# Experts of a routed mixture by items of 64 slots: one item at a time, with rows gathered and scattered per item by GpSimd, in place of rounds of two items side by side

## The chip, the cores and the metric

One core of a Trainium2 chip runs the whole program in one launch. The metric is the device time of that launch in microseconds (us), as the median over repeated runs. All arithmetic is in float32.

## The reference, cut to what matters

The program is four layers: two of one block (three attention and scan branches), then two of a second block, each of which ends in a hierarchical mixture of experts (MoE). The change lies in the two MoE stages, except for one piece of preparation in an attention stage of the first block.

```python
def hier_moe(h, wr_g, br_g, wr_e, br_e, w_gate, w_up, w_down):      # 512 tokens of 1024
    p_group = softmax(xf @ wr_g + br_g);  g_sel = top_k(p_group, 1)        # 4 groups
    fine = (xf @ wr_e + br_e)[chosen group]                                # 8 experts a group
    e_val, e_sel = top_k(fine, 2);  gate = p_top * softmax(e_val)
    ...
    y = (silu(x_rows @ w_gate[e]) * (x_rows @ w_up[e])) @ w_down[e]        # 1024->512, 512->1024
    out[token] += y * gate                                                 # 2 experts a token
x = x + g2 * hier_moe(h, ...)
```

There are 32 experts in a layer, each with three weight matrices of 2 MiB: 96 matrices, 201.3 MB, for each of the two MoE layers. A layer has 512 x 2 = 1024 pairs of token and expert. The reference's own inputs decide how they fall: in the first MoE layer expert 26 gets 69 pairs, expert 29 gets 135 and no other more than 64; in the second only expert 13 has more than 64 (67). In pieces of 64 ("items"), with at least one for each expert, that is 35 items in the first layer (two for expert 26, three for 29) and 33 in the second (two for expert 13).

## The kernel before, in words

A stage of the program is a block in which each of the five engines (TensorE, VectorE, ScalarE, GpSimd, and SyncE, which only issues DMA) runs its own instruction list; a barrier ends it. The MoE of a layer is two stages, `experts` and `moe_residual` (function `experts`).

In `experts`, SyncE first issues six 2 MiB loads (L2898: gate, up and down weights of experts 0 and 1). Meanwhile `route` (VectorE, with two ScalarE exponentials) turns the router's logits into choices, and `plan` ranks the pairs within each expert with TensorE and VectorE and writes a small table `counts` into SBUF, from which each engine later reads loop bounds and expert numbers into registers (`value_load`). The first rows are gathered on TensorE by a product with a one-hot matrix (L427, `pick`). At L2908 GpSimd scatters all token rows, eight indirect DMAs of 128 rows of 4 KB, into the tensor `expert_rows` in device memory, at the seat of each pair.

Then `item_experts` works in rounds. A round has two seats of 64 slots: even experts take seat 0, odd experts seat 1, one after the other, and an expert with more than 64 pairs keeps its seat for further rounds. The number of rounds is the longer of the two seats: 18 in the first MoE layer and 17 in the second. Each seat has its own buffer for gate, up and down weights. A round on TensorE is: gate product of both seats side by side in the two halves of bank 0 (`side_by_side`, L2796), up product into bank 1, transposes of the next round's rows (L2788), transposes of the hidden rows (L2811), down product into banks 4 and 5 (L2796, `experts_wd`). ScalarE does silu (L2840) and moves transposed rows (L2836, L2845), VectorE multiplies (L2861) and scales the result (L2868). SyncE issues the next round's gate loads when the gate product is done, and so on for up and down (L2744), and loads the 128 rows of the next round but one (L2736). GpSimd stores the 128 result rows of 4 KB (L2771) and waits for them to land.

In `moe_residual` GpSimd fetches the results back in token order with eight indirect DMAs of 128 rows (L2927), and VectorE adds them to `x`, weighted (L2952), and makes the next norm (L548, L549, and L2968 in the last layer, which needs the gain `g` loaded at L2939).

Since seats may be partly empty, `expert_rows` is filled with zeros once, by 32 DMAs of 512 KB that GpSimd issues in the first layer's fox attention (L694). In that stage TensorE also computes side products (L726) from weights `side_w` that SyncE loads (L708) into two buffers.

## Time and profile before

| | us |
|---|---|
| median of 3 runs (range) | 4008.1 (4007.0 to 4009.63) |
| the profiled execution's span, first to last instruction | 4008.1 |
| first MoE layer, both stages, about | 2309 to 2909 |
| second MoE layer, both stages, about | 3432 to 4008 |
| TensorE busy over the span | 3480.4 (87%) |

The profiled execution's span is the same as the median, so no time lies around the span that the sum would have to add. A busy share is an average over stages with different limits. The DMA line of the page (mean busy share of the 16 DMA engines, in 40 slices of 100.2 us) shows where transfers are the limit; the MoE stages are the slices 24 to 28 and 35 to 40.

### The profile page before, as it was taken

The page shows a single profiled execution, that of the slowest core. Times are in us where ns is not written, and L with a number is a line of the kernel's source. Part 1 is how long each engine was busy: PE and PEld are TensorE (multiplying, and loading weights), DVE is VectorE, ACT ScalarE, POOL GpSimd, SP SyncE. Part 2 cuts the span into 40 slices and gives each one's busy share as a digit, 9 for nine tenths or more (in the row PEclk, how much of TensorE's full clock was granted, in tenths as well). Part 3 has the DMA queues.
Part 4 walks back from the last instruction along what each step waited for, and adds up shares of the span by engine and source line. Part 5 has one row for each costly group of instructions (what it writes and reads, how often), then busy time and mean ns, then how long its engine had stood idle before and what let it go on. Part 6 is the DMA issues. An engine that isn't in the chain of part 4 may idle for free. (4 is left out here: it accounts for less than half of the span.)

```text
span 4008.1 us, 38008 instructions
## 1 busy us (share of the span) xinstructions
PE 3480.4 (87%) x13936; PEld 1752.2 (44%) x13937; DVE 1688.1 (42%) x3091; ACT 701.3 (17%) x1412; POOL 196.3 (5%) x263
## 2 busy tenths in 40 slices
PE   8998999888899999889889977778699978788775
PEld 4454434885444444378634432223243344422222
DVE  3235556775232555567548420000238766200002
ACT  1132204000112330310010100000122243100001
POOL 0001010001000001000000000000100130000000
PEclk9999999999999999899889989999889989799998
DMA  3115452004121226200143099999533421799996
GB/s 105 68 48 209 143 169 60 1 1 144 47 89 32 68 83 208 55 11 1 59 175 122 0 396 429 428 428 399 202 105 121 110 73 62 310 429 419 429 428 283
DMA packets 208086, 696.40 MB, mean 174 GB/s; under 512 B 22248, under 2 KB 105704, under 8 KB 182608
## 3 DMA queue, kind: packets, MB, share of 16 engines
q1 hardware_dynamic: 178576, 589.56, 38.4%
q0 software_dynamic: 29376, 105.05, 7.2%
q8 instruction: 85, 1.39, 0.2%
q14 instruction: 49, 0.40, 0.0%
HBM read 636.28 MB, written 58.28 MB: 173 GB/s over the span
## 5 line engine op out<-in xcount | busy, mean ns | idle before, releaser
L345 PE MATMUL bank<-fm,w 128*128 128x512 f32 (+1 forms) x912 | 397.3, 596 | 11.4 <-DMA w<-in_ab_w_in 6.3
L2796 PE MATMUL bank<-experts_wu,experts_hs 128*64 128x512 f32 x1120 | 275.8, 650 | 75.0 <-DMA experts_wu<-in_moe_w_up 75.0
L2796 PE MATMUL bank<-experts_wg,experts_hs 128*64 128x512 f32 x1120 | 272.2, 642 | 60.1 <-DMA experts_wg<-in_moe_w_gate 45.6
L345 PE MATMUL bank<-w,fm 128*128 128x512 f32 (+2 forms) x768 | 315.5, 567 | 6.5 <-DMA w<-in_w_in 6.5
L2861 DVE TENSOR_TENSOR fm<-bank,fm 128x512 f32<-128x512 f32 x35 | 37.0, 1056 | 638.9 <-PE bank L2796 638.9
L2796 PE MATMUL bank<-experts_wd,fm 128*64 128x512 f32 x1120 | 256.4, 611 | 45.4 <-issue 24.0
L345 PEld LDWEIGHTS bank<-fm,w 128*128 128x128 f32 (+1 forms) x912 | 172.4, 190 | 234.1 <-issue 221.0
L726 PE MATMUL bank<-fm,side_w 128*128 128x512 f32 x512 | 252.4, 619 | 6.9 <-DMA side_w<-in_w_in 5.4
L345 PEld LDWEIGHTS bank<-w,fm 128*128 128x128 f32 x768 | 142.2, 195 | 179.2 <-issue 153.8
L2796 PEld LDWEIGHTS bank<-experts_wu,experts_hs 128*64 128x64 f32 x1120 | 85.9, 148 | 263.2 <-issue 166.1
L2796 PEld LDWEIGHTS bank<-experts_wg,experts_hs 128*64 128x64 f32 x1120 | 94.6, 147 | 233.6 <-issue 230.5
L2868 DVE TENSOR_TENSOR fm<-bank,mod 128x512 f32<-128x512 f32 x70 | 45.1, 686 | 328.3 <-PE bank L2796 328.3
L427 PE MATMUL bank<-fm,w 128*128 128x512 f32 x384 | 170.3, 599 | 1.6 <-ACT rwkv_a L1362 1.6
L2796 PEld LDWEIGHTS bank<-experts_wd,fm 128*64 128x64 f32 x1120 | 83.7, 140 | 195.7 <-issue 168.3
L843 ACT ACTIVATE prob<-bank,nmax 128x128 f32<-128x128 f32 (+2 forms) x192 | 111.4, 580 | 219.6 <-DVE nmax L891 146.9
L726 PEld LDWEIGHTS bank<-fm,side_w 128*128 128x128 f32 x512 | 91.5, 197 | 91.3 <-issue 83.9
L1944 DVE SCALAR_TENSOR_TENSOR ada_sums<-ada_w,cond,ada_sums 128x1024 f32<-128x1024 f32 x84 | 105.8, 1282 | 37.1 <-DMA ada_w<-in_ada_w 35.9
L2840 ACT ACTIVATE fm<-bank 128x512 f32<-128x512 f32 x35 | 20.9, 597 | 560.2 <-PE bank L2796 560.2
L345 PE MATMUL bank<-w,merged 128*128 128x512 f32 x256 | 113.2, 600 | 3.1 <-DVE merged L1443 3.1
L427 PEld LDWEIGHTS bank<-fm,w 128*128 128x128 f32 x384 | 73.7, 193 | 96.3 <-issue 93.8
L345 PE MATMUL bank<-o_fm,w 128*128 128x512 f32 x240 | 105.8, 600 | 6.3 <-DMA w<-in_w_pc 6.3
L761 PE MATMUL bank<-consts,prob 128*128 128x128 f32 x512 | 78.7, 282 | 30.0 <-ACT pT L826 15.9
(484 smaller groups left out, 4875.5 us busy)
## 6 DMA issues: line engine op xcount, KB each, us to landing
experts_wg<-in_moe_w_gate SPq DMA_DIRECT2D x64, 2048.0 KB, 19.5
experts_wu<-in_moe_w_up SPq DMA_DIRECT2D x64, 2048.0 KB
experts_wd<-in_moe_w_down SPq DMA_DIRECT2D x64, 2048.0 KB
ada_w<-in_ada_w POOLq DMA_DIRECT2D x96, 512.0 KB, 4.9
w<-in_w_in SPq DMA_DIRECT2D x40, 512.0 KB, 3.9
expert_rows<-fm POOLq DMA_DIRECT2D x35, 512.0 KB, 10.3
fm<-expert_rows SPq DMA_DIRECT2D x33, 512.0 KB, 21.6
w<-in_w_in SPq DMA_DIRECT2D x16, 1024.0 KB, 7.2
```

Of the source, the lines that this page charges most:

```text
L345: ins = pe.matmul(bank, lhsT, rhs, start=(n == 0), stop=(n == len(todo) - 1))
L427: last = pe.matmul(out, lhsT, rhs, start=(n == 0), stop=(n == len(pairs) - 1))
L726: last = pe.matmul(SIDE[:, :], side_w[n % 2][:, k_, :], side_h[:, k_, :], start=(k_ == 0), stop=(k_ == DC - 1))
L761: last = pe.transpose(T[n % 2][:, j * P:(j + 1) * P], prob[s % 4][:, j * P:(j + 1) * P], chip.ident)
L843: act.activation(prob[s % 4][:, 0:n], S[s % n_scores][:, 0:n], ACT.Exp, bias=nmax[:, s:s + 1], scale=1.0 if bias is None else -1.0, accum_ ...
L1944: ins = dve.scalar_tensor_tensor(sums, self.slot[n % self.slots][:, :], by, sums, ALU.mult, ALU.add)
L2796: ins = pe.matmul(bank[rows, :], lhs[:, k, rows], weights[:, s, k, cols], start=(k == 0), stop=(k == chunks - 1))
L2840: act.activation(act_out[:, :], B[0][:, :], ACT.Silu).then_inc(*silued.inc())
L2861: dve.tensor_tensor(dealt(hid[:, :], FC), B[1][:, :].rearrange("p (q k) -> p q k", k=FC), act_out[:, :].rearrange("p (q k) -> p q k", k=FC ...
L2868: ins = dve.tensor_tensor(y[:, cols], B[4 + d][:, :], gate_row[:, cols], ALU.mult)
```

## The change

The two seats are given up. Work goes item by item, in the order of the experts, and an item's gate and up products run side by side in the two halves of bank 0, with the same rows as the stationary operand. Its down product comes one item late: in iteration `p` TensorE turns the hidden rows of item `p - 1`, makes gate and up of item `p`, turns the rows of item `p + 1`, and makes the down product of item `p - 1`, whose two column halves lie side by side in bank 4. Gate and up weights have two buffers each, down weights one. SyncE's list is written out for all 32 experts.

GpSimd gathers each item's rows from `token_rows` (the normed tokens, stored there by SyncE in the stage ahead, `keep`) with an indirect DMA of half rows (2 KB), and scatters the results as half rows straight to `made_rows`, in the order of the pairs. Slots without a pair are sent out of bounds (one slot of each half stays), so nothing is moved for them. GpSimd waits for no landing in its loop; VectorE does, before it overwrites `y`. `plan` makes the two index tables `at_from` and `at_to` in place of the scatter positions; the one-hot gather and the zero fill are gone. `moe_residual` reads `made_rows` with eight plain DMAs on SyncE, ahead of the clearing of semaphores and the load of `g`.

```diff
@@ attention (fox attention, first layer)
-                for n in range(cleared_rows.shape[0] // P):
-                    pool.dma_start(cleared_rows[n * P:(n + 1) * P, :], zero[:, :]).then_inc(*wiped.inc(16))
-                pool.wait_ge(*wiped.at(wiped.total))
@@ the stage ahead of experts
+    def keep(self, sp, h):
+        for t in range(TILES):
+            sp.wait_ge(*self.norm.normed.at(t + 1))
+            sp.dma_start(self.chip.token_rows[t * P:(t + 1) * P, :], h[:, t, :]).then_inc(*self.chip.tokens_kept.inc(16))
@@ plan
+            dve.tensor_tensor(at_slot[:, :, half * SLOTS:(half + 1) * SLOTS], over(chip.number, [P, 2 * TILES, SLOTS], 1),
+                              over(own_rank, [P, 2 * TILES, SLOTS], 2), ALU.is_equal)
+        link(dve.tensor_tensor(at_item[:, :, :], over(chip.number[:, 0:ITEMS], [P, 2 * TILES, ITEMS], 1),
+                               over(own_first, [P, 2 * TILES, ITEMS], 2), ALU.is_equal))
+        link(dve.tensor_tensor(at_item[:, :, :], at_item[:, :, :], over(chip.pair_number, [P, 2 * TILES, ITEMS], 2), ALU.mult))
...
+        product(pe, B[3][:, 0:ITEMS], [(at_slot[:, a, :], at_item[:, a, :]) for a in range(2 * TILES)]).then_inc(*tabled.inc())
@@ item_experts, SyncE
+        for e in range(EXPERTS):
+            if e == 2:
+                sp.wait_ge(*counted.at(1))
+            if e >= 2:
+                sp.wait_ge(*first_done.at(at(e - 2, END_AT, 1)))
+            load("moe_w_gate", e, wg[:, e % 2], gate_loaded[e % 2])
+            load("moe_w_up", e, wu[:, e % 2], up_loaded[e % 2])
+            if e == 0:
+                load_down(0)
+            if e >= 2:
+                sp.wait_ge(*down_done.at(at(e - 1, FIRST_AT, 1) + 1))
+                load_down(e - 1)
+        sp.wait_ge(*down_done.at(at(EXPERTS - 1, FIRST_AT, 1) + 1))
+        load_down(EXPERTS - 1)
@@ item_experts, GpSimd
-            pool.wait_ge(*yready.at(p + 1))
-            pool.dma_start(rows[bass.ds(p * P, P), :], y[:, :]).then_inc(*ystored.inc(16))
-            pool.wait_ge(*ystored.at(16 * p + 16))
-            pool.sem_inc(yfree.sem, 1)
+        with pool.Fori(2, n + 2) as q:
+            pool.wait_ge(*rows_turned.at(q - 1))
+            fetch(q - 1, picked_from, q)
+            pool.wait_ge(*y_ready.at(q))
+            pick_to(q - 2)
+            spread(q)
@@ item_experts, TensorE
+        def gate_and_up(p, s):
+            pe.wait_ge(*filled.at(p + 1))
+            for k in range(DC):
+                rows = hs[:, k % 4, k // 4, :]
+                for half, w in ((slice(0, SLOTS), wg), (upper, wu)):
+                    ins = pe.matmul(B[0][half, :], rows, w[:, s, k, :], start=(k == 0), stop=(k == DC - 1))
+            ins.then_inc(*first_done.inc())
...
+                with pe.Fori(first, end) as p:
+                    landed = pe.value_load(counts[0:1, bass.ds(p + DOWN_AT, 1)], min_val=16, max_val=16 * EXPERTS)
+                    turn_hidden(p)
+                    pe.wait_ge(*gate_loaded[s].at(16 * j + 16))
+                    pe.wait_ge(*up_loaded[s].at(16 * j + 16))
+                    gate_and_up(p, s)
+                    turn(p + 1)
+                    pe.wait_ge(*down_loaded.at(landed))
+                    down(p)
@@ item_experts, VectorE
+            dve.wait_ge(*down_done.at(p + 1))
+            dve.wait_ge(*y_stored.at(16 * p + 16))
+            dve.tensor_tensor(y[:, :], B[4][:, :], gate_half[:, :], ALU.mult).then_inc(*y_ready.inc())
@@ experts
+                @st.block.scalar
+                def _(act):
+                    for half in range(2):
+                        rows = slice(half * SLOTS, (half + 1) * SLOTS)
+                        act.activation(gate_half[rows, :], mod[rows, 5, half * BANK:(half + 1) * BANK], ACT.Copy).then_inc(*gated.inc())
                 route(chip, st, lg, choice, weight, routed, routed_ready)
@@ moe_residual
-                    pool.indirect_dma_start(out=rows[:, at, :], out_offset=None, in_=made,
-                                            in_offset=bass.IndirectOffsetOnAxis(ap=row_of[:, at:at + 1], axis=0)
-                                            ).then_inc(*fetched[at].inc(16))
+                    sp.dma_start(rows[:, at, :], chip.made_rows[at * P:(at + 1) * P, :]).then_inc(*fetched[at].inc(16))
                 for c in used:
                     sp.sem_clear(c.sem)
```

On TensorE, the loop over rounds stood so in the instruction list (`fm` holds the hidden and the incoming rows; `ISA`, `REGISTER_ALU` and `COMPARE_AND_BRANCH` are register, wait and loop instructions, `TENSOR_LOAD` a register loaded from the table):

```order
L2824 ISA
L2799 TENSOR_LOAD experts_counts
L2799 ISA x2
L2801 REGISTER_ALU
L2796 MATMUL bank<-experts_wg,experts_hs 64x512 x16
L2796 MATMUL bank<-experts_wu,experts_hs 64x512 x16
L2785 ISA
L2788 MATMUL bank<-consts,fm 128x128 x8
L2811 MATMUL bank<-consts,fm 128x128 x4
L2796 MATMUL bank<-experts_wd,fm 64x512 x16
L2824 REGISTER_ALU
L2824 COMPARE_AND_BRANCH
```

Now what stands between the down product of one expert's last item and the first gate and up products of the next expert is this:

```order
L2813 COMPARE_AND_BRANCH
L2811 ISA
L2811 TENSOR_LOAD experts_counts
L2811 ISA x3
L2811 TENSOR_LOAD experts_counts
L2811 ISA x2
L2813 UNCONDITIONAL_BRANCH
L2813 ISA
L2814 TENSOR_LOAD experts_counts
L2814 ISA x2
L2785 REGISTER_ALU
L2787 MATMUL bank<-consts,fm 128x128 x4
```

One register load per round has become one per item and two more per expert, and the transposes of the hidden rows have moved from ahead of their own item's down product to the start of the next iteration.

On SyncE, the start of the stage was this (loads of both seats, then the loop over rounds):

```order
L2898 DMA experts_wg<-in_moe_w_gate 128x4096 x2
L2898 DMA experts_wu<-in_moe_w_up 128x4096 x2
L2898 DMA experts_wd<-in_moe_w_down 128x4096 x2
L2732 UNCONDITIONAL_BRANCH
L2730 TENSOR_LOAD experts_counts
L2730 ISA x2
```

It is now this, after a first gate load, and goes on in the pattern of the last eight rows to expert 31:

```order
L2712 DMA experts_wu<-in_moe_w_up 128x4096
L2712 DMA experts_wd<-in_moe_w_down 128x4096
L2712 DMA experts_wg<-in_moe_w_gate 128x4096
L2712 DMA experts_wu<-in_moe_w_up 128x4096
L2715 TENSOR_LOAD experts_counts
L2715 ISA x2
L2712 DMA experts_wg<-in_moe_w_gate 128x4096
L2712 DMA experts_wu<-in_moe_w_up 128x4096
L2715 TENSOR_LOAD experts_counts
L2715 ISA x2
L2731 REGISTER_ALU
L2712 DMA experts_wd<-in_moe_w_down 128x4096
```

Five loads instead of six need nothing of the plan, and the down load of an expert stands behind the gate and up loads of the next one.

## Rows read from the trace of the kernel before

**Rows 1.** The page: GB/s moved in 40 slices

```profile
GB/s 105 68 48 209 143 169 60 1 1 144 47 89 32 68 83 208 55 11 1 59 175 122 0 396 429 428 428 399 202 105 121 110 73 62 310 429 419 429 428 283
```

**Rows 2.** Windows: us, busy (count) by engine, granted clock, DMA share, GB/s

```profile
2381.60:2782.00 400.40, 323.36 (x1406) 115.92 (x1404) 30.50 (x39) 28.24 (x52) 6.92 (x13) 0.93 1.01 427
3500.00:3958.00 458.00, 370.88 (x1645) 134.04 (x1643) 35.19 (x45) 33.17 (x61) 7.98 (x15) 0.94 1.01 425
3958.00:3973.00 15.00, 13.66 (x68) 5.18 (x64) 1.35 (x2) 1.57 (x3) 0.00 (x0) 1.00 0.03 12
```

**Rows 3.** DMA queues in 2380 to 2790: packets, MB, share; issues: KB, us to landing

```profile
q1 hardware_dynamic: 13036, 167.86, 96.6%
q0 software_dynamic: 1872, 6.82, 4.1%
...
expert_rows<-fm POOLq DMA_DIRECT2D x13, 512.0 KB, 10.4
```

**Rows 4.** Timeline, TensorE, one round of the first layer's last four

```profile
2846.00 7.04 PE L2796 MATMUL bank<-experts_wg,experts_hs 128*64 128x512 f32 x32
...
2861.06 0.66 PE L2811 MATMUL bank<-consts,fm 128*128 128x128 f32 x4
2862.59 7.09 PE L2796 MATMUL bank<-experts_wd,fm 128*64 128x512 f32 x32 [0.88 <-ACT fm L2845]
```

**Rows 5.** Timeline, TensorE, a product in the stretch where transfers are the limit

```profile
2438.98 8.78 PE L2796 MATMUL bank<-experts_wu,experts_hs 128*64 128x512 f32 x32 [3.84 <-DMA experts_wu<-in_moe_w_up]
```

**Rows 6.** Timeline, start of experts in the first MoE layer

```profile
2301.74 6.88 PE L427 MATMUL bank<-router_w,fm 128*128 128x36 f32 x32
2309.21 0.82 SPq L2898 DMA_DIRECT2D experts_wg<-in_moe_w_gate  x2
2309.22 1.28 ACT L2549 ACT_TABLE_LOAD   x1 [6.16 <-PEq L117]
2310.52 0.22 ACT L2549 ACTIVATE a<-a 128x16 f32<-128x16 f32 x1
2320.92 0.16 DVE L2656 TENSOR_TENSOR place<-place,bank 128x8 f32<-128x8 f32 x1 [2.52 <-PE bank L2623]
2324.73 0.69 DVE L2678 TENSOR_REDUCE rank<-mine 128x16 f32<-128x512 f32 x1
```

**Rows 7.** Timeline, start of experts in the second MoE layer

```profile
3431.85 0.83 SPq L2898 DMA_DIRECT2D experts_wg<-in_moe_w_gate  x2
3459.60 0.23 DVE L2706 CAST experts_counts<-row 1x161 int32<-1x161 f32 x1
3461.32 9.63 PE L2796 MATMUL bank<-experts_wg,experts_hs 128*64 128x512 f32 x32 [6.52 <-issue]
3471.19 1.92 SPq L2744 DMA_DIRECT2D experts_wg<-in_moe_w_gate  x2
```

**Rows 8.** Timeline, the end of a MoE layer, first and then second

```profile
2871.68 0.53 POOL L2771 DMA_DIRECT2D expert_rows<-fm  x1 [22.98 <-DVE fm L2868]
2878.07 0.98 POOL L2927 DMA_INDIRECT rows<-expert_rows,experts_row_of  x1 [5.85 <-POOLq L117]
2882.47 1.28 DVE L2952 SCALAR_TENSOR_TENSOR x<-rows,experts_weight,x 128x1024 f32<-128x1024 f32 x1 [11.46 <-DMA rows<-expert_rows,experts_row_of]
...
3974.66 0.53 POOL L2771 DMA_DIRECT2D expert_rows<-fm  x1 [22.98 <-DVE fm L2868]
3980.95 0.99 POOL L2927 DMA_INDIRECT rows<-expert_rows,experts_row_of  x1 [5.76 <-PEq L117]
3993.16 1.28 DVE L2968 SCALAR_TENSOR_TENSOR rows<-x,norm_ss,g 128x1024 f32<-128x1024 f32 x1
```

**Rows 9.** Timeline, fox attention of the first layer: GpSimd, then TensorE

```profile
357.39 17.08 POOL L694 DMA_DIRECT2D expert_rows<-zero  x32 [0.32 <-POOL zero L691]
...
386.82 3.78 PE L726 MATMUL bank<-fm,side_w 128*128 128x512 f32 x4 [5.35 <-DMA side_w<-in_w_in]
391.50 1.88 PE L726 MATMUL bank<-fm,side_w 128*128 128x512 f32 x4
```

More of the change, by code:

```diff
@@ L2463, in _ @@
             routed.load(sp, io, 1)
+            routed.keep(sp, h)
         @st.block.tensor
@@ L2666, in _ @@
         link(dve.tensor_scalar(blocks[:, :], blocks[:, :], 1.0, None, ALU.max))
-        for seat in range(2):
-            link(dve.tensor_tensor_scan(last[:, seat::2], chip.ones[:, 0:E // 2], blocks[:, seat::2], 0.0, ALU.mult, ALU.add))
-        dve.tensor_tensor(first[:, :], last[:, :], blocks[:, :], ALU.subtract).then_inc(*placed.inc())
-        dve.wait_ge(*placed.at(1))
+        link(dve.tensor_tensor_scan(last[:, :], chip.ones[:, 0:E], blocks[:, :], 0.0, ALU.mult, ALU.add))
+        link(dve.tensor_tensor(first[:, :], last[:, :], blocks[:, :], ALU.subtract))
@@ L2695, in _ @@
-        dve.wait_ge(*tabled.at(1))
-        link(dve.tensor_copy(row[:, EXPERT_AT:EXPERT_AT + ITEMS], B[6][0:1, 0:ITEMS]))
-        begun = B[6][0:1, ITEMS:2 * ITEMS]
-        start, end, landed = (row[:, at:at + ROUNDS] for at in (FROM_AT, TO_AT, LANDED_AT))
-        link(dve.tensor_scalar(end, begun[:, 1::2], 1.0, None, ALU.add))
-        link(dve.tensor_scalar(start, begun[:, 0::2], -1.0, 1.0, ALU.mult, ALU.add))
-        link(dve.scalar_tensor_tensor(start, end, 1.0, start, ALU.subtract, ALU.min))
@@ new lines, in _ @@
+        dve.sem_inc(marked.sem, 1)
+        marked.inc()
+        dve.tensor_copy(row[:, FIRST_AT:FIRST_AT + E], first[0:1, :])
+        dve.tensor_copy(row[:, END_AT:END_AT + E], last[0:1, :])
+        link(dve.tensor_copy(row[:, N_AT:N_AT + 1], last[0:1, E - 1:E]))
+        dve.wait_ge(*tabled.at(1))
+        pairs = B[3][:, 0:ITEMS]
+        dve.tensor_scalar(empty[:, :], pairs, 0.0, None, ALU.is_equal)
+        link(dve.tensor_scalar(where[:, 0, :], pairs, float(SEQ + 1), -float(SEQ), ALU.is_ge, ALU.mult))
@@ L2706, in _, with item_experts @@
+        dve.tensor_copy(at_to[:, 0:1], where[:, 1, ITEMS - 1:ITEMS])
+        dve.tensor_copy(at_to[:, 1:2], where[:, 1, ITEMS - 1:ITEMS]).then_inc(*placed.inc())
+        down = row[:, DOWN_AT:DOWN_AT + ITEMS]
+        link(dve.tensor_tensor(over_by, over(chip.number[0:1, 0:ITEMS], [1, ITEMS, E], 2), over(last[0:1, :], [1, ITEMS, E], 1), ALU.is_gt))
+        link(dve.tensor_reduce(down, over_by, AX.X, ALU.add))
+        link(dve.tensor_scalar(down, down, 16.0, 16.0, ALU.mult, ALU.add))
         dve.tensor_copy(counts[:, :], row[:, :]).then_inc(*counted.inc())
-def item_experts(chip, st, i, io, fm, counts, counted, gate_row, hs, first_filled, rows, rows_written, weights, weights_loaded):
+def item_experts(chip, st, i, io, fm, counts, counted, at_from, at_to, placed, gate_half, gated, hs, weights, loaded):
@@ L2757, in _, with load, at @@
-        load_rows(2)
-        with sp.Fori(2, n) as p:
-            seats = first_two(p)
-            sp.wait_ge(*gathered.at(p))
-            load_rows(p + 1)
-            load("moe_w_down", wd, down_done, down_loaded, p, seats)
+        def load(name, e, into, landed):
+            sp.dma_start(into, io[name][i, e].rearrange("(p k) n -> p k n", p=P)).then_inc(*landed.inc(16))
+        def at(e, where, low):
+            return sp.value_load(counts[0:1, where + e:where + e + 1], min_val=low, max_val=ITEMS - 1)
@@ new lines, in _ @@
+        pool.wait_ge(*placed.at(1))
+        pool.wait_ge(*chip.tokens_kept.at(chip.tokens_kept.total))
+        fetch(0, first_picked, 1)
+        n = items_of(pool)
+        with pool.Fori(2, n + 2) as q:
[4 more added lines that the diff above has]
+            spread(q)
+        for more in range(2):
+            pool.wait_ge(*y_ready.at(n + (2 + more)))
+            pick_to(n + more)
+            spread(n + (2 + more))
@@ new lines, in down @@
+        def down(p):
+            pe.wait_ge(*hmoved.at(p + 1))
+            pe.wait_ge(*y_ready.at(p + 2))
+            for f in range(FC):
+                for d in range(2):
+                    ins = pe.matmul(B[4][d * SLOTS:(d + 1) * SLOTS, :], hidT[:, f, :], wd[:, f, d * BANK:(d + 1) * BANK],
+                                    start=(f == 0), stop=(f == FC - 1))
+            ins.then_inc(*down_done.inc())
+        turn(0)
+        pe.wait_ge(*counted.at(1))
+        with pe.Fori(0, EXPERTS // 2) as j:
+            for s in range(2):
+                first, end = (pe.value_load(counts[0:1, bass.ds(2 * j + (at + s), 1)], min_val=low, max_val=ITEMS - 1)
+                              for at, low in ((FIRST_AT, 0), (END_AT, 1)))
+                with pe.Fori(first, end) as p:
[7 more added lines that the diff above has]
+                    down(p)
@@ L2866, in _ @@
[L2866 to L2871 removed]
+        dve.sem_inc(hidden.sem, 1)
+        dve.sem_inc(y_ready.sem, 2)
+        dve.wait_ge(*gated.at(2))
+        activated(0)
+        scale(0)
+        n = items_of(dve)
+        with dve.Fori(1, n) as p:
+            activated(p)
+            scale(p)
```

323 lines of the change are left out of this document (116 added, 207 removed).

## The prediction

> **What bounds the kernel now.** I read the page's slices first, to find the stretches whose limit is the transfers and not TensorE. In the two MoE stages the DMA engines move 396 to 429 GB/s, slice after slice, and nowhere else do they come near it for long [rows 1]. The windows say it more exactly: over 400 us of the first MoE layer and 458 us of the second, the 16 DMA engines are busy all the time (share 1.01) at 427 and 425 GB/s, while TensorE is busy for 81% of it [rows 2]. So here a byte not moved is time gained, and a moment in which no load is outstanding is time lost; TensorE's work matters only where it lets the queue run dry. The queues of that stretch show what the bytes are: nearly all are SyncE's queue, weights with some row loads; GpSimd's own queue, the row stores in 4 KB pieces, has 6.82 of 174.7 MB (3.9%) and takes 4.1% of the time [rows 3].
>
> The exception is the end of a layer. In the first one the last rounds are limited by TensorE: gate 7.04, up as long, down 7.09, turns, and 0.88 of waiting for ScalarE [rows 4], one round each 23.5 us. In the second, transfers are over at 3958 [rows 2], the last store is issued at 3974.66 and the next stage begins about 3981 [rows 8].
>
> **Transfers removed.** A 2.10 MB weight load at 427 GB/s is 4.9 us; 96 of them are 470.4 us in each layer, before and after. Around them, the second layer moves 8 scatters, 17 stores and 16 loads of 0.524 MB, 21.5 MB, or 50.3 us. Now a layer moves 1024 pairs twice, 8.4 MB, as 4096 pieces of 2 KB. By bytes that is 19.6 us. A 4 KB piece cost 5% more than its bytes [rows 3]; if that is a price per piece, 2 KB pieces cost 10% more: 21.6 us, which I take, because it is nearest to the row. The other end is that a 2 KB piece takes as long as one of 4 KB: 41 us. So the row traffic saves about 29 us a layer, if the queue stays full.
>
> The Trainium skill ("DMA: Bandwidth & Descriptors", Specifications) puts the size below which a piece loses line rate at 512 B. By it the rows would cost 19.6 us instead of 21.6, 4 us less over both layers; no row before has pieces of 2 KB in a full queue, so the trace cannot say.
>
> **The start is where it is given back.** All times now run from a layer's first weight load. Before, six loads and the scatters fill the engines until the first gate product ends, at 3471.19 - 3431.85 = 39.3 us [rows 7]. Now five loads need nothing of the plan and are over at 0.9 + 24.5 = 25.4. The next load waits for the first item's gate and up. Its chain: the ranks are known at 11.7 us [rows 6]. Two new ScalarE copies stand ahead of the table load behind which the exponential waits [rows 6], at 0.6 each, so 12.9. VectorE's chain from 2320.92 to the end of L2678 is 4.5 [rows 6]; less 0.9 for the `pick` steps, plus five short ones, 4.6; then four wide compares of at most 0.69 (L2678's width), about 2.4: 19.9. TensorE's 16 short products at 6.88/32 = 0.215 [rows 6]: 23.3. Ten short VectorE steps of 0.22: 25.5. GpSimd's copy and issue 0.6, the gather 4.4, as the first gather of the residual stage took (2878.07 to 2882.47 [rows 8]): 30.5. Turn 1.0. Three register loads: the first product of before starts 1.5 us after the table is written with two of them [rows 7], so 0.8 each, 2.4. Hidden turn 1.0, and the product at the low clock, 9.63 [rows 7]: 44.5. With 1.1 for issue and first bytes (an estimate) transfers resume at 45.6. The engines idle 20 us.
>
> Then a second gap. Gate and up of expert 2 take until 55.4, but behind them on SyncE's queue stands the down load of expert 1, which waits for the down product of item 0, and that comes after gate and up of item 1: 44.5 + 0.7 + 3.55 + 0.66 + 7.04 + 0.6 + 3.55 = 60.6 (half of a product of 7.04 is 3.55 with its start [rows 4]), bytes at 61.7. 6.3 us more. At 61.7 seven loads are done: 27.4 us lost.
>
> **Between items the queue should stay full, narrowly.** Let T be the landing of the down weights of expert e-2. TensorE began gate and up of e-1 at T - 4.9, ends at T + 2.1, turns, and ends the down product at T + 6.3. Only then is the next down load issued; bytes T + 7.4. The engines are meanwhile on gate and up of e, until T + 9.8 plus 0.7 for the rows. After a wait of 3 us or more the product ran at 8.78 [rows 5], which leaves 1.4 us: the limit for the end of the down product is T + 9.4, and it would end at T + 8. TensorE's item is 11.8 us of work at the high clock; 15.4 are there. I cost this at nothing. Covered too: the gather of the next item has some 15 us, and a store in GpSimd's queue landed in 10.4 under full load [rows 3]; the store of `y` has an item's time before VectorE waits for it.
>
> **An expert with more than one item.** Its buffers are held longer. Count from the landing of expert 13's up weights in the second layer. The queue holds a down load, gate and up of 14, the down load of 13, gate and up of 15 and rows: until 30.6. TensorE makes two items' gate and up, then 14's, with the down products between, and ends the one that frees the buffer at 36.4 (register loads exposed, see below); bytes 37.5. The engines idle 7.0. In the first layer expert 26 costs the same, and from expert 29 on TensorE is the limit.
>
> **The sums.** Second layer: 27.4 + 95 x 4.9 + 21.6 + 7.0 = 521.5 at the landing of expert 30's down weights. The last down load waits for a product and runs alone: product ends +6.3, load landed +12.8, last product +16.4, VectorE and GpSimd's issue 0.9 + 0.6: 539.4. Before, to the issue of the last store: 3974.66 - 3431.85 = 542.8 (the landing behind it is the same). The same arithmetic for before gives 520.7 at the end of transfers where the trace has 526 [rows 2, 7], so it is some 5 short; I add half, 2.7: 542.1, or -0.7. First layer: expert 29's up weights land at 27.4 + 88 x 4.9 + 21 + 7.0 = 486.6; from there TensorE needs 11.2 to its first down product and 11.8 for each of three more items, 46.6; expert 31's gate and up and 30's down product end at 58.4; the last down load has landed at 64.9, the last product ends at 68.5, and at 70 with half of the register loads exposed. 486.6 + 70 + 1.5 + 2.7 = 560.8 against 2871.68 - 2309.21 = 562.5 [rows 6, 8]: -1.7.
>
> The register loads are the place where the Trainium skill speaks against the change: the same page (Latency and other measured facts) gives a floor of about 0.6 us for one, near my 0.8. If all three per expert were exposed, the items where TensorE is the limit would cost 1.4 us more each, about 4 us.
>
> **Outside the experts stage.** The zero fill delays `side_w` in fox attention: 5.35 us of waiting, and the product after it at 3.78 instead of 1.88 [rows 9]: -7.2, and nothing else there hides it, since TensorE has no other gap around it. The plain fetch of the results in place of the indirect one: bytes come some 2.4 us sooner, -2.4 in the first layer. In the last layer `g` is now queued behind eight loads of 1.2 us on SyncE: 1 + 9.8 + 1.2 + 0.8 = 12.8 after the stage's start, and the product that needs it began at 3993.16 - 3980.95 = 12.2 [rows 8]: +0.6 in place of a gain. `keep` writes in a stretch without other transfers: nothing.
>
> Sum: -0.7 - 1.7 - 7.2 - 2.4 + 0.6 = -11.4, from 4008.1 (the execution's own time, equal to the median): **3997**.
>
> **The rivals.** (1) *The forecast*, 3988 to 4006: 40 in 100; about 25 of it below 4000.1. (2) *The starts are cheaper*: the register loads lie under the gather and the plan's compares run faster than 0.69; each of the two layers resumes 6 to 8 us sooner. For it: every step of that chain was priced in series. 3983: 24 in 100. (3) *The single down buffer leaves a gap at each expert*, slower. It decides as soon as the down product ends more than 9.4 us after the landing before it; each 0.5 us beyond costs 0.5 x 58 = 29 us. For it: only 1.4 us are left at 8.78, and a cold one takes 9.63 [rows 7]. Against: once TensorE is late it no longer waits, and without a wait the product takes 7.04 [rows 4]. 4026 and up: 17 in 100. (4) *A 2 KB piece costs as much as a 4 KB one*: 19.4 a layer, 4036. Against: the 5% of [rows 3]. 8 in 100. (5) *The fill's stall is not on the path and the layers come out even*: 4006: 11 in 100.
>
> **Numbers.** What a measurement of this kernel can tell from no change is about 0.2%, 8 us. Faster: 0.25 + 0.24 = 0.49; same: 0.15 + 0.11 = 0.26; slower 0.25. The range leaves out part of (2) below and part of (3) above: 3970 to 4038; the likeliest case's own is 3988 to 4006.
>
> **What would show it.** GB/s zero for about 20 us from 25 us after a layer's first load, and for 6 us at 55; then a share near 1 and one gate and up every 15.3 us; GpSimd's queue at about 4% of the time; TensorE's fox attention without a wait on `side_w`; in the last layer VectorE waiting for `g`. Wrong it would be if the share between items were under 0.97, or the first gap under 12 or over 28 us.

## The result, and the profile after

The change makes the kernel **slower**: median 4063.3 us (4060.7 to 4066.3, 4 runs) against 4007.6 us, ratio 1.0143, 95% interval [1.0122, 1.0163]. The forecast was 3997 with a range to 4038. The profiled execution has a span of 4058.9 us, 50.8 more than before. Where they went, with the forecast of each piece beside it:

| piece of the span, us against before | forecast | measured |
|---|---|---|
| up to the first weight load of the first MoE layer | -7.2 | -9.3 |
| that layer, first load to the issue of the last store of rows | -1.7 | +34.1 |
| from there to the second MoE layer's first load | -2.4 | -9.9 |
| second layer, first load to last store | -0.7 | +30.9 |
| from there to the end | +0.6 | +5.0 |
| sum | -11.4 | +50.8 |

So the loss lies inside the two experts stages, 596.6 and 573.7 us long. The line of slices shows it in the places of [rows 1]:

```profile
GB/s 108 63 47 64 157 135 52 1 1 143 62 72 47 63 149 141 52 1 1 181 50 121 126 347 391 391 389 350 150 98 134 98 73 76 322 396 374 402 395 240
```

In the first layer's full slices 391 stands where 428 stood. The windows of the changed kernel (columns as in [rows 2]: time busy by engine, granted clock, DMA share, GB/s), first the steady stretches of the two layers, then 16 us between two experts, then the two gaps at the start of the first layer:

```profile
2420.00:2700.00 280.00, 216.59 (x940) 78.95 (x938) 28.89 (x33) 25.51 (x49) 41.21 (x67) 0.90 0.95 392
3560.00:3860.00 300.00, 241.16 (x1054) 86.92 (x1052) 32.80 (x37) 29.47 (x56) 45.20 (x74) 0.90 0.95 390
2659.00:2671.00 12.00, 11.84 (x42) 4.09 (x44) 1.08 (x1) 1.19 (x2) 0.19 (x2) 0.74 1.01 427
2671.00:2673.00 2.00, 2.00 (x12) 0.57 (x8) 0.00 (x0) 0.00 (x0) 1.04 (x1) 1.00 0.51 205
2673.00:2675.00 2.00, 2.00 (x12) 0.96 (x12) 0.69 (x1) 0.38 (x1) 0.18 (x1) 1.00 0.56 119
2326.00:2346.00 20.00, 13.53 (x56) 5.31 (x58) 3.71 (x5) 2.17 (x4) 5.29 (x8) 0.71 0.17 50
2356.00:2362.00 6.00, 6.00 (x32) 2.09 (x30) 1.33 (x2) 0.54 (x2) 2.10 (x3) 1.00 0.42 111
```

The share is 0.95, not 1.01: the queue runs dry between items, as the prediction had named for the wrong case (under 0.97). The two gaps at the start are there as forecast. The timeline shows the rhythm, SyncE first, then TensorE in the same stretch:

```profile
2640.22 0.33 SPq L2712 DMA_DIRECT2D experts_wd<-in_moe_w_down  x1
2641.16 0.33 SPq L2712 DMA_DIRECT2D experts_wg<-in_moe_w_gate  x1
2641.53 1.07 SPq L2712 DMA_DIRECT2D experts_wu<-in_moe_w_up  x1
2653.36 0.33 SPq L2712 DMA_DIRECT2D experts_wd<-in_moe_w_down  x1
2654.30 0.33 SPq L2712 DMA_DIRECT2D experts_wg<-in_moe_w_gate  x1
...
2673.43 0.33 SPq L2712 DMA_DIRECT2D experts_wd<-in_moe_w_down  x1
```

```profile
2642.07 0.61 PE L2795 MATMUL bank<-experts_wg,experts_hs 128*64 128x512 f32 x1 [1.30 <-issue]
...
2649.08 0.66 PE L2780 MATMUL bank<-consts,fm 128*128 128x128 f32 x4
...
2659.16 1.08 PE L2795 MATMUL bank<-experts_wg,experts_hs 128*64 128x512 f32 x1 [5.25 <-issue]
...
2669.15 0.66 PE L2780 MATMUL bank<-consts,fm 128*128 128x128 f32 x4
2669.74 3.65 PE L2804 MATMUL bank<-experts_wd,fm 128*64 128x512 f32 x16
```

A down load opens each group of three, and the next group comes 13.1 and 20.1 us later in turn (2640.22, 2653.36, 2673.43). Every second gate and up product waits 5 to 6 us (the profile names no releaser here and says "issue"; both weights are waited for at this place), begins at the low level of the clock (granted 0.50 in the microseconds from 2659 to 2665), and takes longer: 10.0 us here, from 2659.16 to 2669.15, which is the longest of the eight in 2420 to 2700; they take 8.4 to 10.0, 9.1 in the mean. The products between them wait 1.6 us at most and take 7.0 (2642.07 to 2649.08). In the trace's steady stretch of 24 experts, gate loads follow each other at a mean of 16.4 us; the prediction's terms give 15.4. The waits of TensorE in 2420 to 2700 (total, times, longest):

```profile
PE bank L2795 <- issue: 60.9, 16, 6.4
PE bank L2804 <- DMA experts_wd<-in_moe_w_down: 2.5, 5, 0.7
```

The last stage, which answers to the end of [rows 8]:

```profile
4020.43 0.98 POOL L2753 DMA_INDIRECT made_rows<-fm,now_to  x1 [0.84 <-POOL now_to L2748]
4029.18 4.42 SPq L2919 DMA_DIRECT2D rows<-made_rows  x8
4034.66 0.33 SPq L2923 DMA_DIRECT2D g<-in_norm_rows  x1
4044.00 1.28 DVE L2952 SCALAR_TENSOR_TENSOR rows<-x,norm_ss,g 128x1024 f32<-128x1024 f32 x1 [4.52 <-DMA g<-in_norm_rows]
```

### The profile page after: what moved, and what is told of

It reads as the page before. It is cut to its first block and busy times, and to the rows that moved or that the text cites. A ratio compares the mean times of both kernels' runs of the same rounds, so it can differ in the third digit from the quotient of the medians.

```text
span 4058.9 us, 38277 instructions
## 1 busy us (share of the span) xinstructions
PE 3477.0 (86%) x13904; PEld 1745.2 (43%) x13905; DVE 1734.0 (43%) x3122; ACT 734.6 (18%) x1482; POOL 302.5 (7%) x445
## 5 line engine op out<-in xcount | busy, mean ns | idle before, releaser
L2795 PE MATMUL bank<-experts_wg,experts_hs 128*64 128x512 f32 x1088 | 541.2, 655 | 191.0 <-issue 190.9
L2795 PE MATMUL bank<-experts_wu,experts_hs 128*64 128x512 f32 x1088 | 542.2, 656 | 0.0
L346 PE MATMUL bank<-fm,w 128*128 128x512 f32 (+1 forms) x912 | 398.4, 598 | 11.8 <-DMA w<-in_ab_w_in 6.5
L2858 DVE TENSOR_TENSOR fm<-bank,fm 64x512 f32<-64x512 f32 x68 | 72.8, 1071 | 772.7 <-ACT fm L2844 772.7
L2795 PEld LDWEIGHTS bank<-experts_wg,experts_hs 128*64 128x64 f32 x1088 | 158.0, 151 | 506.4 <-issue 506.4
L2844 ACT ACTIVATE fm<-bank 64x512 f32<-64x512 f32 x68 | 40.1, 589 | 706.6 <-PE bank L2795 706.6
L2795 PEld LDWEIGHTS bank<-experts_wu,experts_hs 128*64 128x64 f32 x1088 | 157.8, 151 | 0.0
L2854 DVE TENSOR_TENSOR fm<-bank,experts_gate_half 128x512 f32<-128x512 f32 x70 | 48.4, 692 | 216.4 <-PE bank L2804 216.4
L1894 POOL DMA_DIRECT2D ada_base<-in_ada_b x24 | 12.2, 515 | 1456.9 <-PE bank L346 1450.3
```

The lines of the kernel that those rows point to most:

```text
L346: ins = pe.matmul(bank, lhsT, rhs, start=(n == 0), stop=(n == len(todo) - 1))
L1894: pool.dma_start(self.base[32 * j:32 * j + 32, :], io["ada_b"][l:l + 1, c0:c0 + BANK].to_broadcast([32, BANK])).then_inc(*based.inc(16))
L2795: ins = pe.matmul(B[0][half, :], rows, w[:, s, k, :], start=(k == 0), stop=(k == DC - 1))
L2844: act.activation(act_out[:, :], B[0][0:SLOTS, :], ACT.Silu).then_inc(*silued.inc())
L2854: dve.tensor_tensor(y[:, :], B[4][:, :], gate_half[:, :], ALU.mult).then_inc(*y_ready.inc())
L2858: dve.tensor_tensor(dealt(hid[:, :], FC), B[0][upper, :].rearrange("p (q k) -> p q k", k=FC), act_out[:, :].rearrange("p (q k) -> p q k", ...
```

## The experiments

Twelve kernels ran, in three groups, each on a chip of its own: e1 to e4, e5 to e8, e9 to e12. The kernel before took 4029, 4031 and 4000 us there (4008 in the first comparison), while the changed kernel took 4063.3 in the first comparison and 4058.8 in the third group. In the first two groups it did not run as it is. In the second one e7 stands for it, the changed kernel plus a fill worth 10.2 to 11.7 us: 4070.6, so some 4059 to 4060 without it, where the kernel before took 4031. The edits are edits of the changed kernel, so they are compared with it in us, and differences under some 10 us between groups are not read; the distances of the gate loads inside a trace carry more than the totals. The theories went as the expectations name them: A, the place of the waiting down load on SyncE's queue; B, transfers dearer than priced; C, the lateness hides something; D, too little room for the way back; E, the clock alone.

The time of an expert is the mean distance of gate loads in the first layer, from expert 3 to expert 27 (from expert 8 in e5 and 9 in e11, where the queue is full).

| kernel | median us | ratio to before | us an expert, first layer | DMA share, GB/s, clock in 2420 to 2700 |
|---|---|---|---|---|
| changed | 4063.3 | 1.0143 | 16.4 | 0.95, 392, 0.90 |
| e9 changed again | 4058.8 | 1.0149 | 16.4 | 0.95, 393, 0.91 |
| e1 down load later on the queue | 4063.4 | 1.0089 | 16.3 | 0.97, 394, 0.91 |
| e2 two queues | 4093.2 | 1.0156 | 16.8 | 0.95, 383, 0.89 |
| e3 down product in its own turn | 4064.1 | 1.0070 | 16.2 | 0.98, 402, 0.92 |
| e4 matmuls in the waits | 4047.2 | 1.0042 | 15.6 | 1.00, 415, 1.00 |
| e5 two down buffers | 3983.0 | 0.9887 | 15.5 | 1.01, 424, 0.95 |
| e12 two buffers, old wait | 4055.4 | 1.0127 | 16.2 | 0.98, 402, 0.92 |
| e11 best | 3973.2 | 0.9932 | 15.4 | 1.01, 424, 0.98 |

**e1.** SyncE, the down load one expert later:

```diff
-            if e >= 2:
-                sp.wait_ge(*down_done.at(at(e - 1, FIRST_AT, 1) + 1))
-                load_down(e - 1)
+            if e >= 2:
+                down_up_to(e - 2)      # for the experts with more than one item: ahead of gate and up of e
```

> Edit: one down buffer as before, but SyncE asks for the down weights of expert e-2 behind gate and up of e, so that gate and up no longer stand behind a load that waits for a down product (the experts that have more than one item in this input keep the old place; they are written into the kernel by number). Theory A (the gap comes from the place of the waiting down load on SyncE's queue; in the steady stretch a pair of experts takes 32.8 us where its transfers are 30.6): a pair falls to 30.6 to 31.2, about 1 us for each of some 28 experts in each layer, and the second gap of each start (6 us) goes: 3985 to 4005 us. Theory B (row pieces of 2 KB or the 16 engines are slower than priced, and the gaps are a symptom): a pair stays above 32.2, over 4040 us.

Measured 4063.4 us: no gain, theory A as I had put it is wrong. The trace says why. SyncE, then two down products of TensorE, within 25 us:

```profile
2563.01 0.33 SPq L2712 DMA_DIRECT2D experts_wg<-in_moe_w_gate  x1
2563.39 0.43 SPq L2712 DMA_DIRECT2D experts_wu<-in_moe_w_up  x1
2569.07 0.33 SPq L2712 DMA_DIRECT2D experts_wd<-in_moe_w_down  x1
```

```profile
2565.38 3.65 PE L2810 MATMUL bank<-experts_wd,fm 128*64 128x512 f32 x16 [1.82 <-DMA experts_wd<-in_moe_w_down]
2582.07 5.35 PE L2810 MATMUL bank<-experts_wd,fm 128*64 128x512 f32 x16 [4.84 <-DMA experts_wd<-in_moe_w_down]
```

Now the down product waits for its weights (58.7 us in 18 waits), at the low clock again, and since TensorE works in order the next gate and up, and with it the next gate load, come after it. The wait has moved from one load to another, and the room is the same five buffers. The range for theory B (over 4040) was met, but not its reason: the engines had idle time here too (share 0.97).

**e2.** Gate and up loads issued by ScalarE behind the last silu of expert e-2 and its move of the next rows.

```diff
+            if e + 2 < EXPERTS:
+                for name, into, landed in (("moe_w_gate", wg, gate_loaded), ("moe_w_up", wu, up_loaded)):
+                    act.dma_start(into[:, e % 2], ...).then_inc(*landed[e % 2].inc(16))
```

> Edit: the gate and up loads from expert 2 on are issued by ScalarE, right behind the last silu of expert e-2 (that is when their buffers are free), and SyncE issues the down loads alone. General, no expert is named. Theory A: as e1_order, a pair of experts in 30.6 to 31.2 us, 3985 to 4005 us; ScalarE's two issues and two register loads of an expert (some 2.5 us) lie in its idle time. Theory B: a pair above 32.2 us, over 4040. Third possibility: loads of two queues share the engines, so that gate and up land later than in one queue, and TensorE waits longer at a full queue: share near 1 and yet no gain over 4020.

Measured 4093.2 us, 30 slower than the changed kernel, at 383 GB/s, with a share of 0.95: theory B's range again, but again with idle engines. TensorE waits for the down weights as in e1 (62.5 us in 17 waits, up to 6.2), so a second queue makes no room. The Trainium skill says as much of bandwidth ("DMA: Bandwidth & Descriptors", Issuing engines are not separate DMA queues). Against e1 an expert takes 16.8 us instead of 16.3, and the two experts stages are 11.5 and 17.1 us longer, which is nearly all of the 30; what makes each expert slower was not taken apart.

**e3.** The down product in its own item's turn.

```diff
                     gate_and_up(p, s)
                     turn(p + 1)
-                    pe.wait_ge(*down_loaded.at(landed))
-                    down(p)
+                    turn_hidden(p + 1)
+                    pe.wait_ge(*down_loaded.at(32 * j + 16 * s + 16))
+                    down(p + 1)
```

> Edit: the down product is made in its own item's turn, behind the turn of the next rows, not one item late; loads, buffers and GpSimd's part are unchanged. A down product on an item that does not exist is made at the start, instead of one at the end. Theory A (the lateness of the down product is what closes the loop: up weights, gate and up, the down product of the item before, next down load, and gate and up behind it): gate and up of e+2 are asked for when gate and up of e end, 4 to 8 us earlier, and the queue stays full; TensorE's item is 7.05 + 0.66 + some 3 us of silu, product and hidden turn + 3.65 = 14.5 us at the high clock, just inside 15.3: a pair in 30.6 to 32 us, 3995 to 4030 us. Theory C (the lateness is worth what it hides): TensorE waits 3 us more for each item and 2 more at the low clock, a pair takes 33.5 or more, over 4080 us.

Measured 4064.1 us, between the two ranges, and the same as the changed kernel. TensorE's item is 13.6 us where it does not wait, less than my 14.5, and waits of 36.2 us for down weights (15 times) take the rest. In the total the lateness by itself neither costs nor saves; an expert of the steady stretch takes 16.2 us instead of 16.4.

**e4.** Four matmuls on constants behind each down product.

```diff
                     down(p)
+                    for _ in range(4):
+                        pe.matmul(B[7][:, :], chip.ident, gate_half[:, :], start=True, stop=True)
```

> Edit: four matmuls of 128x512 on constants into a bank that nobody reads (3.4 us at the high clock) behind each down product; nothing else. The output is the same. They keep TensorE busy in most of the 6 us in which it waits for weights, and delay gate and up where it does not wait. Theory A with a share for the clock: the product behind a wait falls from 9.1 to 7.05 us, the alternation of 13.1 and 19.9 us evens out, a pair takes 31.5 to 32, 4010 to 4045 us. If the clock has no share: 4060 to 4080 us.

Measured 4047.2 us, 2 above the range for a share of the clock and 13 under the other one, and in the steady stretch nearly everything comes back. The window of 2420 to 2700 and TensorE's waits in it, and then the same for e5:

```profile
2420.00:2700.00 280.00, 275.16 (x1152) 106.90 (x1150) 31.79 (x36) 28.28 (x54) 43.78 (x72) 1.00 1.00 415
...
PE bank L2795 <- issue: 4.7, 9, 0.9
```

```profile
2420.00:2700.00 280.00, 228.73 (x1010) 79.42 (x1008) 31.18 (x36) 28.25 (x54) 44.07 (x72) 0.95 1.01 424
...
PE bank L2792 <- DMA experts_wu<-in_moe_w_up: 18.1, 12, 1.8
```

With the clock at its high level throughout, the mean matmul of gate and up is 595 ns (666 in the changed kernel), the alternation is gone, the share is 1.00, and an expert takes 15.6 us. The way from the start of a product to the next down load is 11.3 us:

```profile
2556.60 0.61 PE L2795 MATMUL bank<-experts_wg,experts_hs 128*64 128x512 f32 x1 [0.59 <-issue]
...
2567.90 0.33 SPq L2712 DMA_DIRECT2D experts_wd<-in_moe_w_down  x1
```

Doing 3.4 us more work per item made the kernel 12 to 16 us faster. In the first layer the 24 steady experts are 19.3 us shorter together, and 9 us are paid back at its start and behind expert 27. But the edit does two things at once. It holds the clock high, and it lengthens TensorE's item to 15.3 us (2556.60 to 2571.86), as long as an expert's transfers, so TensorE can no longer run ahead in one step and wait in the next. The shorter way is the clock's part; how much an even pace alone would have given, at the low clock, was not tried.

**e5.** As e3, with two buffers of down weights and six loads ahead of the plan.

```diff
-weights: ("wd", [P, FC, D])
+weights: ("wd", [P, 2, FC, D])
+            if e < 2:
+                load_down(e)
+            else:
+                sp.wait_ge(*down_done.at(at(e - 2, END_AT, 1) + 1))
+                load_down(e)
```

> Edit: as e3_now (down product in the item's own turn), and two buffers of down weights instead of one; the down weights of expert e are asked for behind the down product of e-2, six loads stand ahead of the plan. Theory D (what fails is the room between loads asked for and the way back: from the landing of up weights it is 9.1 + 0.7 + 3.65 us and some 2 to the first bytes of the next load, about 15.5, and five buffers leave 11 to 15 behind it; a sixth buffer adds 4.9): the queue stays full between items, share 0.99 or more, 15.3 to 15.6 us an expert instead of 16.4, and no second gap at the start; some 30 us a layer, ratio to the kernel before 0.995 to 1.003. Theory E (only TensorE's low clock behind a wait matters, buffers do not): 16 us or more an expert, ratio 1.006 or more.

Measured 3983.0 us, ratio 0.9887 [0.9853, 0.9921], 76 to 80 us faster than the changed kernel; theory D by its 15.5 us an expert, but better than its range of the ratio. Each layer gives 40 us, not 30: 29.5 up to expert 27, and 10 behind the last gate load, where the changed kernel's last down load comes late and alone. In the window the queue does not run dry (share 1.01), and the longest wait of TensorE for weights is 1.8 us (row above), though the clock is not always high (0.95): with room, the low clock opened no gap there.

**e6.** The four matmuls once per expert, and `g` ahead of the eight row loads.

> Edit: as e4_warm, but the four matmuls on constants stand behind the last item of an expert and not behind each item, so that further items of one expert do not pay for them; and the gain row g of the last layer is asked for ahead of the eight row loads of the last stage. The output is the same. Both theories: 15.5 us an expert as e4_warm, 3.4 us less for each of the four further items (13.6 us where TensorE is the limit, or less), and 2.5 to 4.5 us less at the end. Ratio 0.998 to 1.003, against 1.0042 of e4_warm.

Measured 4036.9 us, 1.0021 [1.0005, 1.0037], as expected. The step of expert 26 with its second item falls from 25.4 to 21.9 us. The last stage, from its first issue to the first store of the output:

```profile
4007.96 0.33 SPq L2921 DMA_DIRECT2D g<-in_norm_rows  x1
4008.34 4.19 SPq L2924 DMA_DIRECT2D rows<-made_rows  x8
4020.92 0.34 SPq L2931 DMA_DIRECT2D out<-rows  x1
```

13.0 us, against 16.1 in the changed kernel and 15.4 in e4: `g` first is worth 2.4 to 3.1.

**e7.** The zero fill of fox attention put back, to a tensor that nobody reads.

> Edit: the changed kernel with the zero fill of fox attention put back (32 stores of 0.52 MB to a tensor that nobody reads). If the fill's stall was on the path: the wait of TensorE on side_w is back, 7 to 9 us over the changed kernel, ratio to before 1.016 to 1.0165. If it was covered: 1.0143, no difference.

Measured 4070.6 us. The ratio (1.0106) says nothing, since the kernel before was slow on that chip. The trace does: TensorE waits 5.36 us for `side_w` and the product after it takes 3.78, both as in [rows 9], and the first MoE load comes at 2312.10, 10.2 to 11.7 us later than in the other three kernels of that group.

```profile
389.54 3.78 PE L727 MATMUL bank<-fm,side_w 128*128 128x512 f32 x4 [5.36 <-DMA side_w<-in_w_in]
```

**e8.** As e4 with nearly no row traffic.

> Edit: as e4_warm (queue full in the steady stretch of the first layer), and all but one slot of each item point outside their tensors, so that the gathers and scatters are issued and move 2 rows of 2 KB each instead of some 60; the residual stage reads the rows of the tokens instead. It leaves out the experts' results, and the second layer then routes other rows, so only its first MoE layer is compared. It prices the row pieces. By bytes an expert is 0.6 us less, at 10% over the bytes 0.7, at the price of a 4 KB piece 1.2 us; e4_warm takes 15.5 us for one there, so 14.9, 14.8 or 14.3. If the engines are no longer the limit at 15.5 us, nothing changes.

Inconclusive: 15.4 us an expert instead of 15.6. With its extra matmuls TensorE's item is 15.3 us, so it had become the limit and hid the price. The base was badly chosen, and e10 repeats it on a base where the transfers are the limit.

**e9.** The changed kernel again.

> Edit: none, the changed kernel once more, as the mark for the other kernels of this call and for e7, since the kernel before takes some 4030 us here where it took 4008. If the ratio is a property of the two kernels: 1.012 to 1.016, some 4088 us. If what the kernel before lost here is its own (its transfers or its clock) and not the changed kernel's: about 4060 us, 1.007 to 1.009, and e7_fill_back was 9 us over it.

Measured 4058.8 us, ratio 1.0149 [1.0132, 1.0166]; the chip was one where the kernel before takes 4000.5. The ratio is the one expected for a property of the two kernels, the time the one expected for the other case, so this run does not decide between them. The verdict repeats; what made the kernel before 20 to 30 us slower on two chips stays open.

**e10.** e5 with nearly no row traffic.

> Edit: e5_two_buffers, whose engines are busy all the time at 15.45 us an expert while TensorE's item is 13.6, with all but one slot of each item pointing outside, so that 2 rows of 2 KB are moved instead of some 60 on average; the last stages read the tokens' rows instead. It leaves out the experts' results; the second layer routes other rows, so only the first MoE layer is compared. It prices the row pieces where the transfers are the limit, which e8 did not. 2 KB pieces at 10% over their bytes: 14.8 us an expert; at their bytes: 14.85; at the price of 4 KB pieces: 14.2, which the loads alone forbid (three of 4.9 are 14.7), so 14.7 and a difference of 0.75 or more.

```profile
2420.00:2700.00 280.00, 235.77 (x1065) 82.92 (x1062) 32.94 (x38) 29.86 (x57) 46.73 (x76) 0.96 1.01 424
```

The engines are still full, and an expert takes 14.88 us (18 of them) instead of 15.46 (19, in e5): the rows of an item cost 0.58 us, where 2 KB pieces at their bytes would be 0.6 (8.1 MB less in a layer, at 424 GB/s). Rival (4), which needs 1.2 us, is out.

**e11.** e5, with ScalarE's gate copies behind `route` and `g` behind the first two row loads.

> Edit: e5_two_buffers, and two small things: ScalarE's two gate copies stand behind its work for the routing instead of ahead of it (1.2 us sooner in each layer's start), and the gain row g of the last layer is asked for behind the first two row loads (e6 saved 2.6 us with it ahead of all eight). 3 to 6 us under e5_two_buffers: ratio 0.984 to 0.989.

Measured 3973.2 us (3971.6 to 3981.1), ratio 0.9932 [0.9919, 0.9946], above the expected range, with a kernel before that is 30 us faster on that chip than beside e5; in us it is 10 under e5 where 3 to 6 were expected, across two groups. It is 86 us under the changed kernel in the same group, 27 under the kernel before. The next gate load of the start comes 43.6 and 42.6 us after the first one, 0.7 sooner than in e5.

**e12.** e5's buffers with e3's wait.

```diff
-            if e < 2:
-                load_down(e)
-            else:
-                sp.wait_ge(*down_done.at(at(e - 2, END_AT, 1) + 1))
-                load_down(e)
+            if e == 0:
+                load_down(0)
+            if e >= 2:
+                sp.wait_ge(*down_done.at(at(e - 2, END_AT, 1) + 1))
+                load_down(e - 1)
```

> Edit: e5_two_buffers with its two buffers of down weights used in turn, but each down load of e asked for only behind the down product of e-1, as with one buffer (and five loads ahead of the plan). One wait differs. Theory D (room): as e3_now, 16 us or more an expert with waits for down weights, ratio 1.004 to 1.010. If e5 won by anything but the room (the other address, the start): well under 1.0.

Measured 4055.4 us, ratio 1.0127 [1.0108, 1.0146], above the expected range of the ratio, beside a fast kernel before; the 16.2 us an expert and the waits for down weights are those of e3. Window and waits as in e4 and e5:

```profile
2420.00:2700.00 280.00, 221.87 (x970) 78.49 (x968) 30.15 (x35) 26.72 (x51) 41.81 (x68) 0.92 0.98 402
...
PE bank L2803 <- DMA experts_wd<-in_moe_w_down: 36.6, 16, 4.4
```

The same arithmetic, the same two buffers, the down load asked for one expert later, and so five loads ahead of the plan instead of six: 72 us over e5, 82 over e11 in its own group. In the first layer the stretch up to expert 27 is 25 us longer than in e5. This is the room; neither the second buffer's address nor the turn of the down product brings any of it.

## Why the prediction was wrong

**The step that failed** is "Between items the queue should stay full, narrowly", costed at nothing. It compared a way back of 14.0 us (from the landing of up weights to the first bytes of the next down load, with the product at 8.78) with a room of 15.4 us, the loads already asked for behind those weights, and found 1.4 us to spare. In the eight long waits of 2420 to 2700 the way from the product's start to the issue of the next down load is 12.7 to 14.3 us, 13.3 in the mean, where the forecast's terms give 12.9 and then 1.1 to the bytes. That side was nearly right. The room was not: counted from the product's start, in windows of half a microsecond, the engines run full for 10.5 to 12.5 us, 11.4 in the mean. At the product of 2659.16, the slowest of the eight, it is 14.3 us of way (product 10.0, turn and down product 4.2, 0.1 to SyncE) against 11.9 us of room, since the engines run full only to about 2671.

The room is short because the product starts later than a count of bytes has its weights landed, and by then part of the loads behind them is already moved. At 2659.16 that is some 3 us, an estimate: three loads and some rows at 427 GB/s, counted back from 2671. The forecast put this at nothing. The last down load of the second layer shows it alone, since nothing stands behind it (SyncE's issue, three windows, then TensorE's product):

```profile
4004.07 0.33 SPq L2712 DMA_DIRECT2D experts_wd<-in_moe_w_down  x1
...
4005.00:4010.00 5.00, 0.00 (x0) 0.00 (x0) 0.00 (x0) 0.04 (x1) 1.18 (x2) 0.66 1.01 360
4010.00:4011.00 1.00, 0.00 (x0) 0.00 (x0) 0.00 (x0) 0.00 (x0) 0.00 (x0) 0.50 0.70 283
4011.00:4012.00 1.00, 0.00 (x0) 0.00 (x0) 0.00 (x0) 0.00 (x0) 0.00 (x0) 0.50 0.15 57
...
4012.70 5.70 PE L2804 MATMUL bank<-experts_wd,fm 128*64 128x512 f32 x16 [8.08 <-DMA experts_wd<-in_moe_w_down]
```

The bytes begin 0.9 us behind the issue. At 427 GB/s they would be over 4.9 us later, at 4009.9; the engines taper off until about 4012, and the product begins at 4012.70, 2.8 us behind the count. The Trainium skill ("DMA: Bandwidth & Descriptors", Anatomy of one DMA) gives a DMA issued by GpSimd a fixed cost of some 2 us, most of it the receipt of the last write; this load is SyncE's, and the trace shows the sum of taper and signal, not the receipt by itself.

**Rival (3) had the mechanism**, the place and the direction, at 17 in 100. Its price of 4026 and up is met by 4063, but its argument against itself ("once TensorE is late it no longer waits, and without a wait the product takes 7.04") describes only every other expert. One item with hardly a wait (a step of 13.1 us) is faster than its transfers (15.4), so the next one waits 5 to 6 us and starts at the low clock (19.9). I had weighed one item at a time, and the loop settles into a pair. 24 experts at 16.4 instead of 15.4 are 24 of the first layer's 36 us over its forecast; expert 26 is 4.6 more (27.0 between gate loads instead of 22.4). At the end of that layer the lone down load takes 9.1 us from its issue to its product instead of 6.5, and the product, at the low clock, 6.65 instead of 3.6: 5.7 more.

**Room and clock.** e5 and e12 give and take the room by one wait, and that is shown: 15.5 us an expert against 16.2. The clock's part is read from e4, which brings 15.6 with five buffers: at the high clock the way to the issue is 11.3 us, and 12.2 with the 0.9 to the bytes, inside the upper part of the 10.5 to 12.5 of room, and at the low clock it is 13.3 and more, outside it. That this alone closes the gap is argued, since e4 also evens TensorE's pace. The Trainium skill describes such a swing ("TensorE: Matmul & The Clock Gate", HAM oscillation): a wait for weights in every step makes each step begin at the low clock. The trace agrees, with the difference that here it is every second step (9.1 us instead of 7.0), and that the price is in the transfers, not in TensorE's own time.

**Right:** the start (20 us idle and then 6; the next gate load at 43.3 us where the product was forecast to end at 44.5, the down load at 59.2 against 60.6); rival (2) is out with that, since only 1 us came back. An item in which TensorE waits for nothing takes the 11.8 us forecast (2785.91 to 2797.68 in the first layer). The register loads, priced at 2.4 us in the start and 1.5 at the end, cost nothing that these rows show: they stand between an expert's last down product and the next hidden turn, and that turn starts at 2640.11, as the down product of 2636.53 ends after its 3.65. The Trainium skill's floor of about 0.6 us for one ("DMA: Bandwidth & Descriptors", Latency and other measured facts) is not contradicted, but the 4 us that exposed loads would have cost do not appear. The row traffic (0.58 us an item measured, 0.68 taken, 0.61 by bytes); by the Trainium skill's rule on pieces of 512 B and more ("DMA: Bandwidth & Descriptors", Specifications) it is their bytes, and e10 agrees. The fill: 7.2 forecast, 10.2 to 11.7 by e7, of which the wait and the slow product after it explain 7.3. `g` with the right sign and too small: the stage's first normalized product comes 14.8 us after its first issue, 12.8 forecast; and the stage starts 8.8 us after the last store instead of 6.3, which was not in the sum.

**Luck, not mechanism:** of the -9.9 between the layers, 11.7 us are the second layer's bias attention (161.9 us in the trace before, 150.2 after). Its code is the same in all kernels, and in the twelve other traces it took 149.2 to 160.3 us. A piece of that size in one pair of profiles is no gain.

**Not tried:** the down product one item late with two buffers; the first item of an expert would use the other slot than its further items.

## What to carry to other kernels

When a change takes away a buffer from a loop that is limited by transfers, count the way back (work at the low clock, issue, first bytes) against the bytes already asked for behind it, less what moves before the landing is seen (some 3 us here), and follow it over two or three steps, not one: a margin of a tenth was no margin, and the layers took 34 and 31 us more. Another queue, or another place on the queue, made no room; asking for one more load ahead did (72 us by one wait), and keeping TensorE busy in its waits shortened the way back, for less (12 to 16 us). Price row pieces where the transfers are the limit: e8, with TensorE at 15.3 us an item, said nothing about them.

## What was not expected of the hardware

Matmuls on constants in the waits made the kernel faster by 12 to 16 us while adding 3.4 us of work to each item: the granted clock went from 0.90 to 1.00 and the moved bytes from 392 to 415 GB/s. Splitting the same loads over two issuing engines cost 30 us, at 383 GB/s. A load that ran alone was ready 2.8 us after a count of its bytes at 427 GB/s. A stretch of unchanged attention code varied by 13 us from trace to trace (149.2 to 161.9). And the kernel before varied by 31 us between chips, while the changed kernel, on the two chips where it ran, stayed within 5.
